# Level products of a block inverse on 32 columns instead of 64, with one masked buffer per level

## The chip, the cores and the metric

One core of a Trainium2 chip runs the whole program. The metric is the device time of one execution in microseconds, as the median of the runs shown. TensorE, VectorE, ScalarE and GpSimd each have their own instruction queue and meet only at semaphores: `wait_ge` holds an engine's queue until a counter is high enough, `then_inc` raises it when an instruction ends.

## The reference, cut to what matters

One layer of a streaming encoder is run on a prompt of 512 frames and a sample of 32. It has chunked attention (8 heads of 64), RWKV-7 time mixing (8 heads of 64), a gated merge and a feed-forward network. The change is in the time mixing, whose recurrence per head is

```
sa = -einsum('bhvk,bhk->bhv', S, kk_t)
S  = S * w_t + sa[..., None] * (kk_t * a_t) + v_t[..., None] * k_t
y_t = einsum('bhvk,bhk->bhv', S, r_t)
```

The state S after each frame depends on the state before it. The kernel doesn't step through frames. It takes chunks of 64 frames; inside a chunk all the `sa` follow from one triangular system with a 64x64 matrix, unit diagonal, and entries made of products of kk, a and the decays. The inverse of that matrix is what the level products compute.

## The kernel before, in words

**Stages.** First come the norm and the input projection in 21 units of weight columns (L1618 to L1693), all through float32r splits (`w_hi`, `w_lo`). Then, from about 339 to 560 us, comes the stage of the change. After it come the state's read-out, the two output projections, the merge and the feed-forward network.

**Units of the stage.** There are NT = 16 units: 4 head pairs (hp) times 4 tiles of 128 frames. A unit holds 2 heads (e) times 2 chunks of 64 frames (c). Chunk c sits on one half of the partitions (`part[c]`), head e on its own 64 columns. A 17th unit (n = NT) does the sample's frames in the same way with 4 levels. Everything of unit n is in buffer set q = n % 2, and its PSUM banks are `bank(q, 0)` to `bank(q, 2)`.

**The order of the stage** is written out by hand, in a loop on each engine over g = 0 .. 127, that is 8 rounds of 16 steps (L1294 on VectorE, L1863 on TensorE). A round takes two units a and b:
- steps 0 and 1: `p_scores` of each (the products that make the triangular matrices, and four transposes), then `v_masks` (L1194) with L1200, L1201, L1204;
- step 2: `p_cv`; step 3 to 12: five levels, each a P step and an X step, each first for a and then for b;
- step 13: `p_wu`, with X as weights; steps 14 and 15: `p_out` for each, and `v_out`.

After each step's work the engine issues a piece of attention (`p_attn`, `v_attn`): scores, transposes and value products of the head pair, 32 steps for each. That is all the filling between the levels. For each head pair after the first, GpSimd prepares the next pair's operands (`prelude`) beside the first round of a pair.

**The levels.** X starts as the inverse on 2x2 diagonal blocks. At level lev, with s = 2 << lev, neighbouring blocks of size s merge into blocks of 2s. In each block of 2s columns the first half is h = 0 and the second h = 1.
- P step (`p_level_p`, L1735): per e and c, one product with ATs as weights (64 columns) and X as moving operand (64 columns) into `bank(q, 2)`. 4 products.
- `v_level_p` (L1215): VectorE multiplies the result for both e by the level's mask into Pb. The mask `lmask[:, lev, :]` is nonzero only in the columns of h = 0. All 64 columns are written, the masked ones with zeros.
- X step (`p_level_x`, L1748): two products for each e and c: X transposed (XT) as weights with Pb moving, and Pb as weights with XT moving. They give the correction to X and to its transpose in `bank(q, 0)`. 8 products; at the last level only the second kind, 4.
- `v_level_x` (L1221): VectorE subtracts from X the columns of h = 0 and from XT those of h = 1, in place. These are all that a level changes.

The waits are a closed ring: the P step waits for `lev_x` of the level before, `v_level_p` for `lev_p_mm`, the X step for `lev_p`, `v_level_x` for `lev_x_mm`. TensorE does a's and b's step behind each other, so b's product runs while VectorE works on a.

A product is one `mm` (L1502, L1503). Matmul and weight load are separate instructions. A float32 product leaves two of each in the records. The two chunks use different quarters of the array and run side by side.

Of the kernel before, what the change touches and what calls it, by code (L numbers as in the profile page):

```python
# [20 lines left out]
ALU = mybir.AluOpType  # L21
AX = mybir.AxisListType.X

P = 128
# [26 lines left out]
def build(nc, x_prompt, x_sample, cache_k, cache_v, state_wkv, state_shift, c_prompt, c_sample, w_ada, b_ada,  # L51
# [6 lines left out]
    L = 64  # L58
# [21 lines left out]
    PERS, HH, HL, XT, RAW, HI, LO, ZS, E = 16512, 20224, 37760, 55296, 72832, 89216, 105600, 121984, 152736  # L80
# [5 lines left out]
    with ctx:  # L86
        def sem(name):
            return ctx.enter_context(nc.semaphore(name))
# [3 lines left out]
        at = lambda name, shape, offset, dt=F32: nc.alloc_sbuf_tensor_at(name, shape, dt, offset=offset)  # L92
# [28 lines left out]
        lmask = at("lmask", [P, 5, L], E + 70208)  # L121
# [32 lines left out]
        def made(q):  # L154
            def row(a, names):
                for n, c, w in names:
                    yield at(f"{n}{q}", [P, c, w], a)
                    a += 4 * c * w
            yield from row((HI, HL)[q], (
                ("ATs", 2, L), ("BDs", 4, L), ("CTs", 2, L), ("XX", 4, L), ("Pb", 2, L), ("KC", 2, P)))  # L160
            yield from row((LO, HL + 4608)[q], (("WU", 2, P), ("tk", 3, P)))
        ATs, BDs, CTs, XX, Pb, KC, WU, tk = zip(made(0), made(1))
        X, XT = [x[:, 0:2] for x in XX], [x[:, 2:4] for x in XX]
        SLOT1 = [a + 8192 + 2208 * i for a in (HI, LO, RAW) for i in range(3)]
        sets = [[at(f"{n}{q}", [P, W + (n == "E1")], a) for n, a in zip(("kt", "bh", "kh", "bl", "kl", "rt", "E1"), places)]
# [65 lines left out]
        hi_done, lo_done, unit_mm = sem("hi_done"), sem("lo_done"), sem("unit_mm")  # L231
# [18 lines left out]
        lev_p = [sem(f"lev_p{q}") for q in range(2)]  # L250
        lev_x_mm = [sem(f"lev_x_mm{q}") for q in range(2)]
        lev_x = [sem(f"lev_x{q}") for q in range(2)]
# [32 lines left out]
        U_OA = U_MG + NG  # L285
# [28 lines left out]
        part = [slice(0, DH), slice(DH, P)]  # L314

        def n_levels(n):

            return 5 if n < NT else 4

        def lev_at(n, lev):  # L320
            return 5 * (n // 2) + lev

        def bank(q, i):

            return ps[:, 3 * q + i, :]

        def squares(b, k, n):

            return b[:, k * L:(k + n) * L].rearrange("p (n c) -> p n c", n=n)

        def both_heads(q, k, n):

            return ps[:, 3 * q:3 * q + 2, k * L:(k + n) * L]

        def sample_out(hp):

            b = (5, 3, 4, 0)[hp]
            return ps[:, b, 256:256 + DH], ps[:, b, 256 + DH:256 + 2 * DH]
# [707 lines left out]
        def _(dve):  # L1046
            link = Chain(dve, dve_c)
            tt, sts, stt = dve.tensor_tensor, dve.tensor_scalar, dve.scalar_tensor_tensor
# [10 lines left out]
            for t, (c0, rows_) in enumerate(TILES):  # L1059
                q = t % 2  # L1060
# [154 lines left out]
            def v_level_p(n, lev):  # L1215
                q = n % 2
                dve.wait_ge(lev_p_mm[q], lev_at(n, lev) + 1)
                tt(Pb[q][:, :, :], squares(bank(q, 2), 4, 2), lmask[:, lev, :].unsqueeze(1).to_broadcast([P, 2, L]),  # L1218
                   ALU.mult).then_inc(lev_p[q], 1)

            def v_level_x(n, lev):  # L1221
                q, s = n % 2, 2 << lev
                dve.wait_ge(lev_x_mm[q], lev_at(n, lev) + 1)
                if lev < n_levels(n) - 1:
                    both = lambda x: bass.AP(tensor=x.tensor, offset=x.offset,
                                             ap=[list(x.ap[0]), [2 * L + s, 2], [2 * s, L // s], [1, s]])
                    x = both(XX[q][:, :, :])
                    tt(x, x, both(bank(q, 0)), ALU.subtract).then_inc(lev_x[q], 1)  # L1228
                else:
                    v = lambda a: a.rearrange("p u (b h s) -> p u b h s", h=2, s=s)[:, :, :, 1, :]  # L1230
                    tt(v(XT[q]), v(XT[q]), v(squares(bank(q, 0), 2, 2)), ALU.subtract).then_inc(lev_x[q], 1)

            def v_out(n):
                (hp, t), q = divmod(n, TT), n % 2
# [31 lines left out]
            def v_own(hp, e):  # L1266

                dve.wait_ge(own_mm, 2 * hp + e + 1)
                if hp:
                    dve.wait_ge(pt_mm, 2 * hp * KS)  # L1270
                low_of(s_sb[0:TS, e, T:T + TS], ps[0:TS, 7, e * TS:(e + 1) * TS],
                       bias[0:TS, hp * 2 + e, T - P:T - P + TS], HUGE, rsum[0:TS, e, 3:4]).then_inc(own_ev, 1)
# [10 lines left out]
            def v_attn(u):  # L1283
                hp, p = divmod(u, 32)
                if hp == HP:
                    return
                if head_at(p, 2, 1):
                    v_scale(hp, *head_at(p, 2, 1))
                if head_at(p, 0):
                    v_scores(hp, *head_at(p, 0))  # L1290
                if p in A_PV[0:2]:
                    v_own(hp, A_PV.index(p))

            for g in range(16 * NR_):  # L1294
                rnd, p = divmod(g, 16)
                a, b = 2 * rnd, 2 * rnd + 1
# [56 lines left out]
            for hp in range(HP):  # L1353
                om, on = sample_out(hp)
                stt(MT4[:, hp, :], dg2[:, :], e4[:, hp:hp + 1], om, ALU.mult, ALU.add)
                i = dve.tensor_copy(NN4[:, hp, :], on)
# [12 lines left out]
            for m in range(HP):  # L1369
# [4 lines left out]
                q = 2 * (m % 3)  # L1374
# [13 lines left out]
            for m in range(HP + 1):  # L1388
                if m < HP:
                    y, g = zs[:, 2 * HP + m, 1:W + 1], gring[:, (KD + m) % 3, :]  # L1390
                    o = sqy[m % 2]
# [40 lines left out]
            for k in range(KD):  # L1432
                i, j = k // 2, k % 2
# [7 lines left out]
                a = tmp_a[:, j, :]  # L1441
# [44 lines left out]
            for t, (_, rows_) in enumerate(TILES):  # L1486
                q = Y_PAIR[t]
                dve.wait_ge(ysq_done, t + 1)
                c = stat[0:rows_, t:t + 1]
# [5 lines left out]
                v = lambda a: a.rearrange("p (b c) -> p b c", b=2)  # L1495
# [5 lines left out]
        def _(pe):  # L1501
            def mm(out, lhsT, rhs, start=True, stop=True):  # L1502
                return pe.matmul(out, lhsT, rhs, start=start, stop=stop)  # L1503
# [11 lines left out]
            for t, (_, rows_) in enumerate(TILES):  # L1515
                if t >= 2:
                    pe.wait_ge(xt_free, t - 1)
                q = t % 2
                for k in range(KD):
                    o = ps[:, 2 * q + k // 4, (k % 4) * P:(k % 4) * P + rows_]  # L1520
                    i = pe.transpose(o, x_block(t, k), ident[0:rows_, 0:rows_])  # L1521
# [134 lines left out]
            for g in range(NG):  # L1656
# [8 lines left out]
                if g < HP:  # L1665
# [3 lines left out]
                    for h in range(2):  # L1669
                        for j in range(2):  # L1670
                            rank = slice(j * DH, (j + 1) * DH)
                            ins = mm(ps[:, 4 + 2 * j + h, 0:H], wup[rank, g * P:(g + 1) * P],
                                     zs[rank, ZT - 2, 1 + h * H:1 + (h + 1) * H])
# [9 lines left out]
                if g in (4, 5):  # L1683
                    for m in range(2 * g - 8, 2 * g - 6):
                        pe.wait_ge(kksq, m + 1)
                        for h in range(2):
                            ins = mm(ps[32 * h:32 * h + 32, 4, 0:H], ind[:, m, :], pz[:, m % 2, h * H:(h + 1) * H],
                                     m == 0, m == HP - 1)
# [46 lines left out]
            def p_level_p(n, lev):  # L1735
                q = n % 2
                if lev == 0:
                    pe.wait_ge(x0_done, n + 1)
                    pe.wait_ge(at_ev, n + 1)
                    pe.wait_ge(cv_ev, n + 1)  # L1740
                else:
                    pe.wait_ge(lev_x[q], lev_at(n, lev))
                for e in range(2):
                    for c in range(2):
                        ins = mm(bank(q, 2)[part[c], (4 + e) * L:(5 + e) * L], ATs[q][part[c], e, :], X[q][part[c], e, :])
                ins.then_inc(lev_p_mm[q], 1)

            def p_level_x(n, lev):  # L1748
                q = n % 2
                pe.wait_ge(lev_p[q], lev_at(n, lev) + 1)  # L1750
                o = bank(q, 0)
                for e in range(2):
                    if lev < n_levels(n) - 1:
                        for c in range(2):
                            mm(o[part[c], e * L:(e + 1) * L], XT[q][part[c], e, :], Pb[q][part[c], e, :])
                    for c in range(2):
                        ins = mm(o[part[c], (2 + e) * L:(3 + e) * L], Pb[q][part[c], e, :], XT[q][part[c], e, :])
                ins.then_inc(lev_x_mm[q], 1)

            def p_wu(n):  # L1760
# [102 lines left out]
            for g in range(16 * NR_):  # L1863
                rnd, p = divmod(g, 16)
                a, b = 2 * rnd, 2 * rnd + 1
# [72 lines left out]
            ins = p_chunks(0, [slice(32 * hp, 32 * hp + 32) for hp in range(HP)], *zip(*[sample_out(hp) for hp in range(HP)]))  # L1938
# [11 lines left out]
            for m in range(HP):  # L1950
                q = 2 * (m % 3)
# [7 lines left out]
                for e in range(2):  # L1959
                    ins = mm(ps[part[e], q + 1, 0:TS], SS[part[e], NCH + 1, m, :], zs[part[e], m, 1 + S0:1 + W])  # L1960
                ins.then_inc(y_mm, 1)

            for m in range(HP):
# [4 lines left out]
                b = 2 * ((m + 1) % 3)  # L1968
                for h in range(2):
                    ins = mm(ps[:, b + h, 0:H], bones[:, :], zs[:, 2 * HP + m, 1 + h * H:1 + (h + 1) * H])  # L1970
# [3 lines left out]
            for m in range(HP):  # L1974
                pe.wait_ge(ysq, m + 1)
                for h in range(2):
                    ins = mm(ps[32 * h:32 * h + 32, 4, 0:H], ind[:, m, :], sqy[m][:, h * H:(h + 1) * H],
                             m == 0, m == HP - 1)
# [57 lines left out]
            for k in range(KD):  # L2036
# [3 lines left out]
                for t, m in enumerate((1, 0)):  # L2040
                    c = k * UW + m * P
                    for j, (w, x) in enumerate(((w_hi, hh), (w_hi, hl), (w_lo, hh))):
                        for h in range(2):
                            ins = mm(ps[:, 2 * t + h, 0:H], w[:, U_UP % 2, c:c + P],
                                     x[:, k, h * H:(h + 1) * H], k == 0 and j == 0, k == KD - 1 and j == 2)
# [25 lines left out]
            u, n = U_DN + 2 * KD - 2, T_DN + KD - 1  # L2071
# [3 lines left out]
            for h in range(2):  # L2075
                for c in range(KDN):
                    hi, lo = ah[:, KDN + c, h * H:(h + 1) * H], al[:, KDN + c, h * H:(h + 1) * H]
                    for j, (w, x) in enumerate(((w_hi, hi), (w_hi, lo), (w_lo, hi))):
                        ins = mm(ps[:, 2 + h, 0:H], w[:, (U_DN + 1) % 2, c * P:c * P + P], x, False, c == KDN - 1 and j == 2)
# [42 lines left out]
```

## Time and profile before

| | us |
|---|---|
| median of 3 runs (1108.6 to 1109.32) | 1108.92 |
| the profiled execution | 1111.06 |
| its span, from first to last instruction | 1109.1 |

| engine | busy us | share |
|---|---|---|
| TensorE, matmul | 1049.9 | 95% |
| TensorE, weight load | 973.4 | 88% |
| VectorE | 393.1 | 35% |
| ScalarE | 346.1 | 31% |
| GpSimd | 369.7 | 33% |

Busy time is the union of an engine's instructions. A matmul's record includes its way through the array, so the TensorE figure isn't the share of its peak. The granted clock (PEclk) is 1 where TensorE ran at 2.4 GHz and 0.5 where it ran at 1.2 GHz; a value between is a mean over a stretch. The mean over the whole run was 0.981.

### The profile page before, as it was taken

The numbers are of one execution on the slowest core, as the hardware profiler recorded it, in microseconds if no ns is written. First come the engines' busy times: TensorE is split into PE (matmuls) and PEld (weight loads), VectorE is DVE, ScalarE is ACT, GpSimd is POOL, SyncE is SP. The second block draws the span as 40 slices with busy tenths as digits, with TensorE's granted clock in tenths as the row PEclk, the third lists the DMA queues.
The fourth block names the chain that finished last, engine by engine and source line by source line (L and its number), as shares of the span: only waits on it lengthen the run. The fifth ranks groups of instructions, "written<-read, shape, count | busy, mean of one in ns | idle before, by whom it ended". The sixth has DMA issues, their size and how long they took to land.

```text
span 1109.1 us, 25395 instructions
## 1 busy us (share of the span) xinstructions
PE 1049.9 (95%) x11052; PEld 973.4 (88%) x11052; DVE 393.1 (35%) x912; ACT 346.1 (31%) x614; POOL 369.7 (33%) x252
## 2 busy tenths in 40 slices
PE   6899999999998989888898899999999999999996
PEld 5699999999997767776796899999999999999996
DVE  2500000086036666666547766322222222100003
ACT  4521222243333444444232323322322232211112
POOL 0555443343315060500231142343343334343340
PEclk9899999999999989899998999999999999999999
DMA  9786756233411000021242432223322322232312
GB/s 368 259 274 232 266 198 205 95 123 132 138 42 46 12 12 22 3 98 76 78 138 72 127 95 77 77 76 105 84 76 76 108 80 64 60 98 82 100 53 81
DMA packets 117180, 122.21 MB, mean 110 GB/s; under 512 B 5428, under 2 KB 102880, under 8 KB 113640
## 3 DMA queue, kind: packets, MB, share of 16 engines
q1 hardware_dynamic: 111872, 111.86, 31.3%
q10 hardware_dynamic: 5224, 9.10, 2.5%
q8 instruction: 69, 1.13, 0.4%
q14 instruction: 15, 0.12, 0.0%
HBM read 108.33 MB, written 15.23 MB: 111 GB/s over the span
## 4 chain that ended last, share of the span: by engine, by line
PE 87%; DVE 8%; issue 2%; ACT 1%; POOL 1%; DMA 1%; SPq 0%; DVEq 0%; ACTq 0%; POOLq 0%
PE ps L1503 83%; PE ps L1823 2%; DVE s_sb L1247 1%; DMA xtok_s<-in_x_sample 1%; PE ps L1723 1%; POOL w_lo L579 1%; DVE y_sb L1496 1%; DVE s_sb L1281 1%; PE ps L1521 1%; DVE mt L1418 0%; DVE Pb L1218 0%; DVE XX L1228 0%; DVE sqy L1395 0%; DVE sq_a L1092 0%; DVE sqy L1399 0%
## 5 line engine op out<-in xcount | busy, mean ns | idle before, releaser
L579 POOL TENSOR_TENSOR w_lo<-w_raw,w_hi 128x2048 fp32r<-128x2048 f32 (+1 forms) x67 | 287.2, 4287 | 565.1 <-ACT w_hi L728 565.1
L1503 PE MATMUL ps<-hh,w_hi 128*128 128x274 f32 x1376 | 291.5, 293 | 5.4 <-DVE hl L1097 4.0
L1503 PE MATMUL ps<-hh,w_lo 128*128 128x274 f32 x1376 | 289.6, 292 | 0.0
L1503 PE MATMUL ps<-hl,w_hi 128*128 128x274 f32 x1376 | 288.1, 291 | 0.0
L1503 PEld LDWEIGHTS ps<-hh,w_hi 128*128 128x128 f32 x1376 | 219.6, 190 | 13.9 <-issue 11.5
L1503 PEld LDWEIGHTS ps<-hl,w_hi 128*128 128x128 f32 x1376 | 219.5, 190 | 0.0
L1503 PEld LDWEIGHTS ps<-hh,w_lo 128*128 128x128 f32 x1376 | 219.2, 191 | 0.0
L728 ACT ACTIVATE w_hi<-w_raw 128x2048 fp32r<-128x2048 f32 (+1 forms) x67 | 119.3, 1781 | 105.0 <-PE ps L1503 99.2
L1503 PE MATMUL ps<-ah,w_hi 128*128 128x274 f32 x352 | 75.3, 290 | 0.3 <-POOL w_lo L579 0.3
L1503 PE MATMUL ps<-ah,w_lo 128*128 128x274 f32 x352 | 75.5, 291 | 0.0
L1503 PE MATMUL ps<-al,w_hi 128*128 128x274 f32 x352 | 75.3, 290 | 0.0
L1503 PEld LDWEIGHTS ps<-ah,w_hi 128*128 128x128 f32 x352 | 56.5, 189 | 0.5 <-POOL w_lo L579 0.5
L1503 PEld LDWEIGHTS ps<-ah,w_lo 128*128 128x128 f32 x352 | 56.6, 190 | 0.0
L1503 PEld LDWEIGHTS ps<-al,w_hi 128*128 128x128 f32 x352 | 56.5, 190 | 0.0
L1024 ACT ACTIVATE ah<-ff_a 128x548 f32 (+1 forms) x22 | 14.6, 662 | 133.8 <-DVE ff_a L1465 133.8
L1461 DVE TENSOR_TENSOR ff_a<-ps,rstd 128x548 f32<-128x548 f32 x22 | 16.0, 728 | 113.7 <-PE ps L1503 113.6
L1428 DVE SCALAR_TENSOR_TENSOR xT<-ps,mod,xT 128x274 f32<-128x274 f32 (+1 forms) x15 | 7.5, 501 | 108.1 <-PE ps L1503 108.1
L1503 PE MATMUL ps<-XX,Pb 64*64 64x64 f32 x672 | 41.8, 228 | 2.6 <-DVE Pb L1218 2.6
L1503 PEld LDWEIGHTS ps<-XX,ATs 64*64 64x64 f32 x672 | 26.2, 145 | 17.9 <-issue 10.4
L1503 PE MATMUL ps<-Pb,XX 64*64 64x64 f32 x536 | 37.7, 236 | 3.0 <-DVE Pb L1218 1.7
L657 POOL TENSOR_TENSOR oal<-qk,oah 128x548 fp32r<-128x548 f32 x4 | 5.4, 1356 | 104.6 <-ACT oah L932 104.6
L1503 PE MATMUL ps<-XX,ATs 64*64 64x64 f32 x672 | 33.9, 238 | 6.6 <-ACT KC L878 3.0
(356 smaller groups left out, 1479.6 us busy)
## 6 DMA issues: line engine op xcount, KB each, us to landing
w_raw<-in_w_ffn_in SPq DMA_DIRECT2D x44, 512.0 KB, 4.7
w_raw<-in_w_in SPq DMA_DIRECT2D x42, 512.0 KB, 5.0
ada_l<-in_w_ada SPq DMA_DIRECT2D x16, 1024.0 KB, 6.3
ada_w<-in_w_ada SPq DMA_DIRECT2D x8, 1024.0 KB, 14.1
w_raw<-in_w_ffn_out SPq DMA_DIRECT2D x16, 384.0 KB, 4.0
gring<-g_d SPq DMA_DIRECT2D x20, 274.0 KB, 2.9
w_raw<-in_w_ffn_out SPq DMA_DIRECT2D x16, 320.0 KB, 3.4
g_d<-gst SPq DMA_DIRECT2D x16, 274.0 KB, 2.6
```

Source lines behind the costliest of these rows:

```text
L579: pool.tensor_tensor(w_lo[:, s, 0:cols], w_raw[:, s, 0:cols], w_hi[:, s, 0:cols].bitcast(F32), ALU.subtract).then_inc(lo_done, 1)
L728: act.activation(w_hi[:, s, 0:cols], w_raw[:, s, 0:cols], ACT.Copy).then_inc(hi_done, 1)
L1024: act.activation(ah[:, i - U_UP, :], ff_a[:, :], ACT.Copy).then_inc(ah_done, 1)
L1247: return dve.tensor_tensor_reduce(out=out, in0=x, in1=y, scale=-1.0, scalar=first, op0=ALU.add, op1=ALU.min, accum_out=low)
L1281: sts(v, v, rsum[0:rows_, e, 2:3], None, ALU.mult).then_inc(p_scaled, 1)
L1428: link(stt(xa[:, 0:H], ps[:, 2 * q, 0:H], g(0), xa[:, 0:H], ALU.mult, ALU.add))
L1461: tt(halves(ff_a[:, :]), pair(1), halves(rstd2[:, :]), ALU.mult).then_inc(pair_free, 1)
L1496: stt(v(y_sb[0:rows_, t, :]), ps[0:rows_, 2 * q:2 * q + 2, :], c, v(gf_row[0:rows_, :]), ALU.mult, ALU.mult).then_inc(yt_done, 1)
L1503: return pe.matmul(out, lhsT, rhs, start=start, stop=stop)
L1521: i = pe.transpose(o, x_block(t, k), ident[0:rows_, 0:rows_])
L1723: ins = pe.transpose(bank(q, 2)[:, i * P:(i + 1) * P], x, ident[:, :])
L1823: ins = pe.transpose(ps[:, 6 + e, b * rows_:(b + 1) * rows_], s_sb[0:rows_, e, b * P:(b + 1) * P], ident[0:rows_, 0:rows_])
```

## The change

The changed code does the following.

- P step: the moving operand is `half(X, lev, 0)`, the 32 columns of h = 0, picked with a stepped access pattern. The results lie densely, 32 columns for each e, in PSUM.
- `v_level_p`: reads the 32 dense columns for each e, multiplies by the half of the mask, and writes only the columns of h = 0 of a masked buffer.
- Each level has a masked buffer of its own, `Pl[q][lev]`; level 0 uses the old Pb. The columns of h = 1 are cleared once, before the loop, by VectorE (10 memsets of 128x2x64, behind a wait for the 21 units of the input projection), and nothing writes them after that.
- X step: the first kind moves the 32 columns of h = 0 of the masked buffer, with all 64 columns of XT as weights. The second kind has all 64 columns of the masked buffer as weights and moves the 32 columns of h = 1 of XT. Results are again dense.
- `v_level_x`: same elements of X and XT as before; the PSUM operand is dense.

The new buffers use space behind the units' small tiles (HI + 4608) and at RAW.

```
+        Pl = [[Pb[q]] + [at(f"Pl{q}{lev}", [P, 2, L], a + 512 * (lev - 1)) for lev in range(1, 5)]
+              for q, a in enumerate((HI + 4608, RAW))]
...
+        def half(x, lev, h):
+            return x.rearrange("p (b h s) -> p b h s", h=2, s=2 << lev)[:, :, h, :]
...
 def v_level_p(n, lev):
-                tt(Pb[q][:, :, :], squares(bank(q, 2), 4, 2), lmask[:, lev, :].unsqueeze(1).to_broadcast([P, 2, L]),
-                   ALU.mult).then_inc(lev_p[q], 1)
+                sides = lambda x: x.rearrange("p e (b h s) -> p e b h s", h=2, s=2 << lev)[:, :, :, 0, :]
+                m = half(lmask[:, lev, :], lev, 0)
+                tt(sides(Pl[q][lev][:, :, :]), bank(q, 2)[:, 4 * L:5 * L].rearrange("p (e b s) -> p e b s", e=2, s=2 << lev),
+                   m.unsqueeze(1).to_broadcast([P, 2] + list(m.shape[1:])), ALU.mult).then_inc(lev_p[q], 1)
...
 before the loop of VectorE
+            dve.wait_ge(unit_mm, U_OA)
+            for b in Pl[0] + Pl[1]:
+                i = dve.memset(b[:, :, :], 0.0)
+            link(i)
...
 def p_level_p(n, lev):
-                        ins = mm(bank(q, 2)[part[c], (4 + e) * L:(5 + e) * L], ATs[q][part[c], e, :], X[q][part[c], e, :])
+                        ins = mm(bank(q, 2)[part[c], 4 * L + 32 * e:4 * L + 32 * e + 32], ATs[q][part[c], e, :],
+                                 half(X[q][part[c], e, :], lev, 0))
...
 def p_level_x(n, lev):
-                            mm(o[part[c], e * L:(e + 1) * L], XT[q][part[c], e, :], Pb[q][part[c], e, :])
+                            mm(o[part[c], 32 * e:32 * e + 32], XT[q][part[c], e, :], half(b[part[c], e, :], lev, 0))
-                        ins = mm(o[part[c], (2 + e) * L:(3 + e) * L], Pb[q][part[c], e, :], XT[q][part[c], e, :])
+                        ins = mm(o[part[c], L + 32 * e:L + 32 * e + 32], b[part[c], e, :], half(XT[q][part[c], e, :], lev, 1))
```

`mm(out, lhsT, rhs)`: the second argument is the weights, the third moves.

## Rows read from the trace of the kernel before

**Rows 1.** The page: granted clock in 40 slices; the chain by line.
```profile
PEclk9899999999999989899998999999999999999999
...
PE ps L1503 83%; PE ps L1823 2%; DVE s_sb L1247 1%; DMA xtok_s<-in_x_sample 1%; PE ps L1723 1%; POOL w_lo L579 1%; DVE y_sb L1496 1%; DVE s_sb L1281 1%; PE ps L1521 1%; DVE mt L1418 0%; DVE Pb L1218 0%; DVE XX L1228 0%; DVE sqy L1395 0%; DVE sq_a L1092 0%; DVE sqy L1399 0%
```

**Rows 2.** Instructions on tile XX; names are out<-moving,weights; duration min/median/max ns, first and last start.
```profile
L1503 PE MATMUL ps<-XX,ATs x672: 217/219/367, 345.3 to 549.1; 64*64 64x64 f32 x168
...
L1503 PE MATMUL ps<-XX,Pb x672: 217/218/312, 346.3 to 551.6; 64*64 64x64 f32 x168
...
L1503 PE MATMUL ps<-Pb,XX x536: 213/219/367, 346.2 to 547.7; 64*64 64x64 f32 x179
...
L1228 DVE TENSOR_TENSOR XX<-XX,ps x67: 268/286/293, 347.4 to 548.1; 128x128 f32<-128x128 f32 x67
...
L1231 DVE TENSOR_TENSOR XX<-XX,ps x17: 201/220/222, 359.4 to 551.9; 128x64 f32<-128x64 f32 x17
```

**Rows 3.** Instructions on tile lmask, the masked copy.
```profile
L1218 DVE TENSOR_TENSOR Pb<-ps,lmask x84: 268/290/293, 345.8 to 549.3; 128x128 f32<-128x128 f32 x84
```

**Rows 4.** Windows: the level stretches, busy us of each engine, clock, DMA.
```profile
345.20:360.90 15.70, 15.44 (x268) 11.87 (x270) 9.26 (x40) 4.55 (x15) 11.12 (x12) 0.89 0.01 3
370.00:384.90 14.90, 13.53 (x263) 10.18 (x260) 10.34 (x42) 4.79 (x12) 0.00 (x0) 1.00 0.07 20
395.00:411.50 16.50, 15.56 (x256) 11.88 (x258) 10.00 (x41) 3.61 (x13) 13.36 (x21) 0.79 0.01 3
...
447.20:463.10 15.90, 15.44 (x246) 12.04 (x247) 8.52 (x32) 3.08 (x10) 11.76 (x20) 0.73 0.01 3
...
497.50:511.20 13.70, 12.17 (x247) 9.45 (x248) 7.45 (x34) 3.08 (x10) 0.00 (x0) 1.00 0.50 208
...
sum 118.20, PE 109.91 PEld 85.24 DVE 74.51 ACT 35.36 POOL 41.00; mean PE 13.74 PEld 10.65 DVE 9.31 ACT 4.42 POOL 5.12
```

**Rows 5.** The same eight windows, instructions on tile XX alone.
```profile
sum 118.20, PE 75.54 PEld 64.06 DVE 20.61; mean PE 9.44 PEld 8.01 DVE 2.58
```

**Rows 6.** Waits from 339 to 543 us: total us, times, longest.
```profile
PEld ps L1503 <- DVE Pb L1218: 10.0, 20, 0.8
...
PE ps L1503 <- DVE Pb L1218: 4.2, 9, 0.6
```

**Rows 7.** The chain in order of time: start us, us, what, records.
```profile
386.57 3.12 PE ps L1503 x156
...
396.61 1.08 PE ps L1503 x32
...
447.22 1.90 PE ps L1503 x32
```

**Rows 8.** TensorE in order of time: start us, us; rows*columns of weights, rows x moving columns.
```profile
345.29 0.68 PE L1503 MATMUL ps<-XX,ATs 64*64 64x64 f32 x16 [1.69 <-ACT KC L878]
...
387.36 0.66 PE L1503 MATMUL ps<-pt_sb,vcs 128*64 128x32 f32 x16
```

**Rows 9.** In order of time before the first mask; a VectorE memset by form.
```profile
338.45 0.10 POOL L653 MEMSET E<- 128x1 f32 x1 [21.24 <-PE ps L1503]
...
340.70 0.29 DVE L1200 TENSOR_TENSOR CTs<-ps,strictU 128x128 f32<-128x128 f32 x1 [3.43 <-PE ps L1723]
...
L1051 DVE MEMSET sc<- 128x256 f32 x1 | 0.3, 272 | 0.9 <-PEq L2106 0.9
```

**Rows 10.** Windows of 5 us around two falls of the clock, and one without.
```profile
380.00:385.00 5.00, 4.03 (x85) 2.71 (x80) 4.75 (x21) 1.71 (x5) 0.00 (x0) 1.00 0.01 3
440.00:445.00 5.00, 3.77 (x88) 2.80 (x80) 4.53 (x11) 3.95 (x15) 3.54 (x3) 1.00 0.17 50
445.00:450.00 5.00, 3.94 (x52) 3.19 (x54) 3.63 (x13) 1.55 (x5) 4.78 (x7) 0.54 0.00 0
...
590.00:595.00 5.00, 2.31 (x16) 1.22 (x14) 4.06 (x6) 0.72 (x2) 0.00 (x0) 1.00 0.28 64
595.00:600.00 5.00, 2.87 (x10) 1.92 (x10) 4.47 (x7) 1.13 (x2) 0.00 (x0) 0.56 0.36 104
```

More of the change, by code:

```diff
@@ L1224, in v_level_x @@
                 if lev < n_levels(n) - 1:
[L1225 to L1228, printed above, removed]
-                else:
-                    v = lambda a: a.rearrange("p u (b h s) -> p u b h s", h=2, s=s)[:, :, :, 1, :]
-                    tt(v(XT[q]), v(XT[q]), v(squares(bank(q, 0), 2, 2)), ALU.subtract).then_inc(lev_x[q], 1)
+                    x = XX[q][:, :, :]
+                    x = bass.AP(tensor=x.tensor, offset=x.offset,
+                                ap=[list(x.ap[0]), [2 * L + s, 2], [2 * s, L // s], [1, s]])
+                    tt(x, x, bank(q, 0)[:, 0:2 * L].rearrange("p (u b s) -> p u b s", u=2, s=s), ALU.subtract)\
+                        .then_inc(lev_x[q], 1)
+                else:
+                    x = XT[q].rearrange("p e (b h s) -> p e b h s", h=2, s=s)[:, :, :, 1, :]
+                    tt(x, x, bank(q, 0)[:, L:2 * L].rearrange("p (e b s) -> p e b s", e=2, s=s), ALU.subtract)\
+                        .then_inc(lev_x[q], 1)
             def v_out(n):
@@ L1750, in p_level_x @@
                 pe.wait_ge(lev_p[q], lev_at(n, lev) + 1)
-                o = bank(q, 0)
+                o, b = bank(q, 0), Pl[q][lev]
                 for e in range(2):
```

## The prediction

> **What bounds the kernel now.** I read the page first. TensorE carries 83% of the chain that ended last, by one line, L1503, the helper through which every product goes, and its granted clock is full in most slices, with short falls in and just before the middle of the run [rows 1]. The changed code runs only in the stage from 339 to 560 us, so I then asked for that stage alone. There the view by tile gives the level products: 672 records that have X as moving operand against ATs, 536 that move the masked buffer and 672 that hold it, each 64 columns wide, in all 1880 records, two for each of 940 products, as every float32 product leaves two [rows 2]. The same view gives the VectorE side: 84 masked copies of 290 ns, 67 subtractions of 286 ns and 17 of 220 ns [rows 2, 3].
>
> The windows over the eight level stretches (each serves two units) say what the stage waits for. The eight take 118.2 us; TensorE is busy for 109.9 of it, VectorE for 74.5 [rows 4]. 75.5 us of TensorE's are products with XX [rows 5], so 34.4 us are other work: attention's scores, transposes and value products that the written order puts between the levels. TensorE bounds the stretches, and VectorE's latency opens short gaps: 29 waits for the masked copy, 10.0 + 4.2 = 14.2 us together [rows 6].
>
> The views of time and of the chain say what one step costs. The X step of two units is 32 records in 1.08 us where the clock is full, and 1.90 us in a stretch at the lower one [rows 7]. The first stretches of three of the four head pairs had a mean clock of 0.89, 0.79 and 0.73 and took 15.7, 16.5 and 15.9 us; the first stretch of the last head pair kept 1.00 and took 13.7; so did the second stretch of every pair, of which one is shown [rows 4]. At 1 for 2.4 GHz and 0.5 for 1.2 GHz those means are 2 x (0.11 x 15.7 + 0.21 x 16.5 + 0.27 x 15.9) = 19 us at 1.2 GHz, and they cost up to 2.0 + 2.8 + 2.2 = 7.0 us.
>
> **The change, part by part.** Nothing is removed from TensorE's list: 940 products, 1880 records, 940 pairs of weight loads, all still there. Each moves 32 columns instead of 64. The weights stay 64 columns wide: ATs, X transposed, and the masked buffer, whose untouched half must be zero because all 64 of its columns are still loaded; that is what the fixed zeros are for.
>
> *The products at full clock.* The trace has a near twin of the new form, attention's 128x32 products with 64 weight columns, also two tiles side by side: 16 records in 0.66 us. Sixteen level records of 64 moving columns take 0.68 us [rows 8]. Half the stream bought 0.02 us per group, and it is bought once, at an end of the group, since in between a pair waits for its weights. So the products themselves gain nothing in their middle. Bounds: 0, or the pace of the stream, 0.54 us less per 32 records; I take 0.02 us for each group that someone waits for, since the twin has the same two counts of columns.
>
> The Trainium skill (TensorE: Matmul & The Clock Gate, section LDWEIGHTS) says that a weight load takes time by its columns alone. [...]
>
> *VectorE.* The masked copy goes from 128 to 64 elements a partition. L1231 is a 128x64 operation on the same operands: 220 ns against 290 [rows 2, 3]. That is 70 ns x 84 = 5.9 us of VectorE's time, which is worth nothing where TensorE is busy. It is on the path at the 29 waits: 29 x (0.07 + 0.02) = 2.6 us, and the next thing late there is the product before it. Bounds: 0 and 5.9; I take -2. The subtractions keep their 128 and 64 elements; the source is now dense and not strided: 0. The half-view that writes or streams runs of 2 to 32 elements is not in the trace for TensorE; the nearest are VectorE's strided subtractions at the price of the dense masked copy, 286 against 290 ns, so 0, up to a few microseconds if TensorE minds short runs.
>
> *The clearing.* Ten memsets of 128x128 stand on VectorE behind a new wait for the last of the input projection's 21 units, which GpSimd's L653 waits for too, until 338.45 us [rows 9]. Behind them is the first mask, for which TensorE waits. That mask starts at 340.70, after 3.43 us of idle time. A memset of 128x256 took 272 ns, so ten of half the size are at most 1.4 to 2.7 us, in a gap of 2.25 [rows 9]. GpSimd copies small tiles in the same gap and could hold VectorE up. Cost 0; if the cover goes, about +1.
>
> *The clock.* This is the term that decides. What TensorE did before it fell is in the windows: from 440 to 445, at full clock, it was busy 3.77 of 5 us with 88 records, then ran 445 to 450 at 0.54. From 380 to 385 it was busy 4.03 us with 85 records and kept the clock, and so did the following stretch [rows 10]. So level stretches stand close to where the clock falls. Now 69% of TensorE's work in them (75.5 of 109.9) has its stream halved. If a shorter stream counts as less work, more of the level stretches run at 1.2 GHz. The trace has neither the case nor its size: bounds are the 19 us at 1.2 GHz of now and the whole 118 us. I take 60 us, half of it, since the steps with attention's wide scores between them still look as they do now, and those without look emptier than what preceded a fall.
>
> What that costs is not what it costs now. A level product with 32 columns at 1.2 GHz streams as long as one of 64 at 2.4 GHz, which its weights hide (if the loads are not slower there; else up to the 1.90 us of today). So levels cost 1.08 us per step at either clock, and only the other work doubles. (a) 41 us more at 1.2 GHz, in which other work is 34.4 of 118.2, that is 0.29 at full clock: 41 / 1.29 x 0.29 = +9. Bounds 0 and +34. (b) The low clock outlives the last level step and reaches the W/U and output products, which are dense: 156 records in 3.12 us [rows 7]. In half of the eight rounds for some 3 us, of which 1.5 is lost: 4 x 1.5 = +6; bounds 0 and 8 x 3.1 = +25. (c) In the 19 us that are already low the level products stop paying: 0.69 x 7.0 = -4.8; some of the 7.0 is GpSimd's and VectorE's shared time, so -4; bounds 0 and -7.
>
> The Trainium skill's same page (HAM oscillation) says that the gate takes the clock away after too little activity and that the penalty then comes on every round. The falls in the trace agree in kind; no row here shows that columns are what it counts.
>
> **Sum.** +9 + 6 - 4 - 2 + 0 = +9 us. The profiled execution took 1111.06 us with a span of 1109.1; what lies around the span stays, so it would be 1120. The median of the runs shown is 1108.92, 2.1 below it, so the forecast is 1108.92 + 9 = 1118.
>
> **Rivals.**
> 1. *The clock stays as it is* (the gate does not mind shorter streams). Then only (c) and VectorE's term are left: -4 - 2, 1103 us. For it: the fall after 595 us came behind 5 us in which TensorE was busy for only 2.31, emptier than any level stretch [rows 10]. Against it: the level stretches with 246 to 268 records at 0.73 to 0.89 are not empty, and fell.
> 2. *The products follow their columns.* 1880 records are 940 pairs at 1.08 / 16 = 0.068 us; half of it on some 60% of the pairs that bound, 0.034 x 940 x 0.6 = -19, with the two gains of rival 1: 1084 us. Against it: 0.66 against 0.68 us [rows 8].
> 3. *Clock and gains cancel*: 1.2 GHz for only some 20 us more, (a) +4.5, (b) +2, less 6: 1109 us.
> 4. *The clearing is not covered*: GpSimd's copies, and its longer operations after, hold each memset, and the first round is late by 3 us while the clock stays: 1106. It matters only beside another case.
>
> **How the numbers follow.** The forecast has 0.6, rival 1 has 0.21, rival 2 has 0.05, rival 3 has 0.12, rival 4 has 0.02. The forecast's own range is 1112 to 1128 by its bounds' nearer halves; the clock falling nearly everywhere would give 1108.92 + 20 to 25. To hold 8 in 10 the range reaches over rival 3 and into rival 1: 1102 to 1127. About 0.2%, 2.2 us, can be told from no change. Faster by more: rivals 1, 2 and 4 and a little of the third, 0.28. Within: 0.14. Slower: 0.58.
>
> **What would show it.** PEclk in the eight level stretches: mean well under 0.9 in most of them, also in the second stretch of each head pair, which is 1.00 now. If these keep 1.00, the clock theory is wrong. The X step of 32 records should still be about 1.08 us at full clock; 0.6 would be rival 2. At the low clock it should be near 1.1 and not 1.9. The masked copy should read 220 ns. The first mask should still start near 340.7. The forecast is wrong in size if the time at 1.2 GHz is far from 60 us in these stretches, or if that time costs less than 0.2 us for each microsecond of it.

## The result, and the profile after

The changed kernel takes 1136.93 us (median of 4 runs, 1135.34 to 1145.82), the kernel before 1109.12 beside it. The ratio is 1.0252, 95% interval 1.022 to 1.0283: slower by 2.5%, some 28 us. The forecast was 1118, slower by 9 us; the sign and the cause held, the size was a third. The profiled execution took 1135.37 us with a span of 1133.7, which is 24.6 us longer than before. TensorE's mean granted clock fell from 0.981 to 0.950.

The page after, granted clock in 40 slices; it answers to [rows 1]:

```profile
PEclk9999999999995969696999899999999999999999
```

There are four dents, one for each head pair; the shallow fifth, the 8 in slice 23, has its like in slice 22 of the kernel before. The windows after, over the eight level stretches: length, then busy us (and records) of TensorE, weight load, VectorE, ScalarE and GpSimd, then the clock. Each stretch runs from a round's first P product to its first W/U product:

```profile
344.30:367.40 23.10, 22.51 (x260) 17.18 (x260) 9.32 (x39) 4.55 (x14) 12.32 (x20) 0.50 0.01 2
378.90:392.90 14.00, 12.69 (x265) 10.32 (x263) 9.87 (x42) 4.78 (x11) 0.00 (x0) 1.00 0.05 15
401.70:423.30 21.60, 19.38 (x256) 14.94 (x256) 10.71 (x41) 4.68 (x15) 14.45 (x22) 0.59 0.01 2
434.50:448.40 13.90, 12.60 (x262) 10.24 (x261) 9.81 (x42) 4.78 (x11) 0.00 (x0) 1.00 0.04 12
459.80:479.40 19.60, 18.68 (x254) 14.58 (x254) 9.51 (x41) 4.61 (x15) 13.62 (x21) 0.59 0.01 2
490.10:505.60 15.50, 14.19 (x263) 11.40 (x261) 9.79 (x42) 4.78 (x11) 0.00 (x0) 0.89 0.05 13
514.50:533.20 18.70, 18.19 (x256) 14.27 (x256) 8.09 (x40) 3.57 (x12) 0.00 (x0) 0.60 0.45 185
544.10:557.10 13.00, 11.70 (x260) 9.54 (x259) 9.17 (x40) 6.59 (x12) 4.67 (x1) 1.00 0.01 3
sum 139.40, PE 129.94 PEld 102.48 DVE 76.28 ACT 38.34 POOL 45.06; mean PE 16.24 PEld 12.81 DVE 9.53 ACT 4.79 POOL 5.63
```

The stretches of [rows 4] were cut a little differently, so here is the kernel before with the new cut, the four first stretches, one second stretch and the sum:

```profile
345.30:360.40 15.10, 14.93 (x258) 11.33 (x259) 8.78 (x39) 4.45 (x15) 10.63 (x11) 0.89 0.01 3
370.70:385.10 14.40, 13.03 (x265) 10.33 (x263) 10.38 (x42) 4.78 (x11) 0.00 (x0) 1.00 0.04 12
393.90:411.00 17.10, 15.52 (x256) 11.71 (x256) 10.68 (x41) 4.71 (x15) 14.39 (x22) 0.80 0.01 3
...
444.40:462.60 18.20, 16.52 (x254) 12.60 (x254) 10.90 (x41) 4.67 (x15) 14.40 (x22) 0.72 0.01 2
...
496.00:510.70 14.70, 12.64 (x254) 9.70 (x254) 8.54 (x40) 3.64 (x13) 0.00 (x0) 1.00 0.58 236
...
sum 121.70, PE 110.72 PEld 85.88 DVE 79.66 ACT 38.40 POOL 44.17; mean PE 13.84 PEld 10.74 DVE 9.96 ACT 4.80 POOL 5.52
```

The two have the same products, and their record counts differ by three at most in a stretch. The four first stretches grew by 8.0, 4.5, 1.4 and 4.0 us and ran at 0.50 to 0.60. The second stretches at full clock got shorter, 14.4 to 14.0 us: that is what the change earns where the clock doesn't move. From clock and length, 2 x (1 - clock) x length, the level stretches now have 75 us at 1.2 GHz against 20. That is 55 more for 17.7 us of length, 0.32 us lost for each. The rest of the 24.6 us, 6.9, lies outside the level stretches. 6.1 of it is in the gaps between the stretches, which had a clock of 1.00 before and have some 16 us at 1.2 GHz now. The gap that grew most, by 2.6 us, is this one:

```profile
448.40:459.80 11.40, 10.67 (x248) 9.17 (x246) 4.85 (x17) 6.01 (x27) 3.65 (x3) 0.70 0.09 26
```

The chain after, in order of time (start, us, line, records), shows the price of one X step and of the output products:

```profile
345.74 1.85 PE ps L1518 x32
...
394.34 3.12 PE ps L1518 x156
...
449.89 5.40 PE ps L1518 x156
...
461.72 1.05 PE ps L1518 x32
```

An X step of 32 records takes 1.05 us at full clock and 1.85 at the low one, where 64 columns took 1.08 and 1.90 [rows 7]. Half the stream is worth 3% at either clock. The output products took 3.12 us at full clock and 5.40 in a fall. The windows of the same stretches confirm the clock:

```profile
345.74:347.59 1.85, 1.85 (x33) 1.78 (x33) 0.87 (x3) 0.30 (x2) 1.79 (x4) 0.50 0.00 0
461.72:462.77 1.05, 1.05 (x33) 0.94 (x32) 1.05 (x2) 0.28 (x1) 0.99 (x2) 1.00 0.00 0
449.89:455.29 5.40, 5.40 (x158) 5.04 (x158) 1.47 (x8) 1.83 (x13) 0.00 (x0) 0.50 0.18 52
```

VectorE's side after, by tile, and then in order of time before the first mask:

```profile
L1226 DVE TENSOR_TENSOR Pl<-ps,lmask x67: 201/225/227, 348.6 to 572.3; 128x64 f32<-128x64 f32 x67
```

```profile
338.40 0.58 DVE L1306 MEMSET Pl<- 128x128 f32 x4
339.65 0.29 DVE L1206 TENSOR_TENSOR CTs<-ps,strictU 128x128 f32<-128x128 f32 x1 [0.66 <-PE ps L1738]
```

The masked copy takes 225 ns, not 290. The clearing ends at 338.98 (338.40 + 0.58) and the first mask still waits 0.66 us for TensorE: it costs nothing.

### The profile page after: what moved, and what is told of

Read it like the earlier page. It is cut to its first block, busy times and chain, and to the rows that moved or that the text cites. A ratio compares the mean times of both kernels' runs of the same rounds, so it can differ in the third digit from the quotient of the medians.

```text
span 1133.7 us, 25406 instructions
## 1 busy us (share of the span) xinstructions
PE 1075.5 (95%) x11052; PEld 996.0 (88%) x11052; DVE 389.5 (34%) x922; ACT 346.2 (31%) x614; POOL 370.2 (33%) x252
## 4 chain that ended last, share of the span: by engine, by line
PE 86%; DVE 7%; issue 2%; DMA 2%; SPq 1%; ACT 1%; POOL 1%; DVEq 0%; ACTq 0%; POOLq 0%
PE ps L1518 83%; PE ps L1839 2%; DMA ada_w<-in_w_ada 2%; SPq L445 1%; DVE s_sb L1257 1%; PE ps L1738 1%; DVE s_sb L1291 1%; POOL w_lo L585 1%; DVE y_sb L1511 1%; DVE mt L1433 0%; DVE XX L1236 0%; DVE sq_a L1098 0%; DVE gring L1431 0%; DVE hl L1103 0%; PE ps L1627 0%
## 5 line engine op out<-in xcount | busy, mean ns | idle before, releaser
L1518 PEld LDWEIGHTS ps<-hh,w_hi 128*128 128x128 f32 x1376 | 218.8, 190 | 14.2 <-issue 10.5
L1518 PEld LDWEIGHTS ps<-XX,ATs 64*64 64x64 f32 x672 | 30.5, 166 | 18.3 <-issue 12.3
L1518 PE MATMUL ps<-XX,ATs 64*64 64x32 f32 x672 | 36.4, 250 | 6.6 <-ACT KC L884 2.9
L1518 PE MATMUL ps<-XX,Pl 64*64 64x32 f32 x536 | 39.7, 255 | 2.4 <-DVE Pl L1226 2.4
## 6 DMA issues: line engine op xcount, KB each, us to landing
ada_w<-in_w_ada SPq DMA_DIRECT2D x8, 1024.0 KB, 14.1
```

## The experiments

The first three experiments test the cause against a rival: A, shorter streams take the clock down; B, VectorE's new work costs the time.

**e1: full streams, everything else of the change.** The edit, in part in words:

```
 def p_level_p   (changed kernel)
-    mm(bank(q, 2)[part[c], 4 * L + 32 * e:4 * L + 32 * e + 32], ATs[q][part[c], e, :], half(X[q][part[c], e, :], lev, 0))
+    mm(bank(q, 2)[part[c], (4 + e) * L:(5 + e) * L], ATs[q][part[c], e, :], X[q][part[c], e, :])
 def v_level_p
-    source: bank(q, 2)[:, 4 * L:5 * L], dense
+    source: sides(squares(bank(q, 2), 4, 2))
 def p_level_x
-    both kinds move half(..., lev, h)
+    both kinds move all 64 columns; v_level_x as before
```

> The changed kernel with the streams of all level products put back to 64 columns; the masked buffers with fixed zeros, their clearing and VectorE's masked copy of 64 elements stay. Theory A (the shorter streams lower the granted clock): the clock of the stage returns to about 0.95 to 1.00, the X step of 32 records is 1.08 us there, and the time is that of the kernel before less up to 3 us for the shorter masked copy: 1106 to 1109 us. Theory B (the cost is VectorE's: clearing, stepped writes, more buffers): it stays at 1130 us or more, since all of that is still in.

Measured: 1108.11 us, ratio 0.9993 (0.9979 to 1.0008), mean clock 0.981. Theory B is out: the clearing, the masked buffers and VectorE's shorter copy are all still in. The level stretches of e1, the four first ones and the sum:

```profile
347.00:362.00 15.00, 14.86 (x260) 11.46 (x260) 8.52 (x39) 4.54 (x14) 10.59 (x11) 0.89 0.01 3
...
395.20:411.10 15.90, 14.04 (x254) 10.66 (x254) 10.61 (x41) 4.70 (x15) 14.34 (x22) 0.89 0.01 3
...
444.30:461.30 17.00, 15.19 (x255) 11.67 (x255) 10.58 (x41) 4.66 (x14) 14.32 (x22) 0.80 0.01 2
...
494.40:507.50 13.10, 12.45 (x256) 9.59 (x256) 8.09 (x40) 3.65 (x13) 0.00 (x0) 1.00 0.66 267
...
sum 116.40, PE 107.23 PEld 83.86 DVE 76.41 ACT 38.49 POOL 44.00; mean PE 13.40 PEld 10.48 DVE 9.55 ACT 4.81 POOL 5.50
```

**e2 and e3: one step at a time.** e2 is e1 with the P step's 32 columns of the change; e3 is e1 with the X step's.

> The changed kernel with 32 columns in the P step alone (336 of 940 products); the X step streams 64. Theory A, with the stream as what counts: about a third of the dose, so the clock between 0.95 and 0.98 over the whole run and a time of 1110 to 1122 us; with steps, as the clock has two levels only, it need not be in proportion. Theory B: 1130 us or more, with the clock of the changed kernel.

> The changed kernel with 32 columns in the X step alone (604 of 940 products); the P step streams 64. Theory A: about two thirds of the dose: 1118 to 1132 us, more than the variant with the P step alone. Theory B: as the changed kernel, 1130 us or more, and no different from the P step alone.

Measured: e2 1117.97 us, ratio 1.0092 (1.0047 to 1.0138); e3 1129.2 us, 1.0171 (1.0143 to 1.02). The order and the sizes are A's. The sum over the level stretches and the longest of them, first of e2, then of e3:

```profile
445.40:465.20 19.80, 17.73 (x256) 13.87 (x256) 10.49 (x41) 4.66 (x14) 14.39 (x22) 0.66 0.01 2
...
sum 121.10, PE 111.58 PEld 88.14 DVE 75.66 ACT 38.33 POOL 44.11; mean PE 13.95 PEld 11.02 DVE 9.46 ACT 4.79 POOL 5.51
```

```profile
451.20:472.90 21.70, 20.20 (x256) 15.65 (x256) 10.22 (x41) 4.72 (x15) 14.40 (x22) 0.56 0.01 2
...
sum 136.20, PE 127.06 PEld 99.51 DVE 76.17 ACT 38.42 POOL 44.05; mean PE 15.88 PEld 12.44 DVE 9.52 ACT 4.80 POOL 5.51
```

In the four kernels with these masked buffers the span rises with the time at 1.2 GHz. Time at 1.2 GHz in the whole span, 2 x (1 - mean clock) x span, against the span:

| kernel | mean clock | span us | at 1.2 GHz | over e1: span / low time |
|---|---|---|---|---|
| e1, streams of 64 | 0.981 | 1105.5 | 42 | |
| e2, P step 32 | 0.972 | 1111.8 | 62 | 6.3 / 20 = 0.31 |
| e3, X step 32 | 0.954 | 1127.4 | 104 | 21.9 / 62 = 0.35 |
| changed, both 32 | 0.950 | 1133.7 | 113 | 28.2 / 71 = 0.40 |

The price isn't quite constant, 0.31 to 0.40. Single executions agree: the slowest of e2 had a clock of 0.955 and a span of 1126.5 us, nearly those of e3's profiled one, 0.954 and 1127.4. The same clock goes with the same span, whichever step has the short stream.

One rival stands untested. In every run with 32 moving columns they are picked by a stepped pattern, so their number and the step weren't changed apart. The step doesn't slow the products (1.05 against 1.08 us), but no run here moved 32 adjacent columns.

**e4 and e11: more work to hold the clock.** e4 adds to the changed kernel, e11 the same to the kernel before, in the first round of each head pair:

```
 p_level_p: for _ in range(4 if lev == 0 and n in (0, 1, 4, 5, 8, 9, 12, 13) else 1):   # the 4 products
 loop:      after the P step of b at levels 1 to 4: mm(ps[:, 1, 320:512], ident[:, :], bias[:, 0, 0:192])
            (left out in one place, g = 9)
```

The repeated P products move 32 columns in e4 and 64 in e11.

> The changed kernel with more work for TensorE, in the first round of each head pair: the P products of level 0 are issued four times instead of once, and behind the P step of each later level stands one product of 192 columns whose result nobody reads. That is about 4 x (4 x 0.32 + 2 x 0.7) = 11 us more of TensorE's work at full clock, some of it in gaps. Theory A: the clock of these rounds rises from 0.50 to 0.76 towards 1, and the time falls though there is more work: 1115 to 1128 us. Theory B, or any cause that is not the clock: the time rises by 5 to 11 us, to 1140 or more.

> The price of the added work: the kernel before with the same additions as the changed kernel had in the filler experiment (level 0's P products four times in the first round of each head pair, one product of 192 columns behind the P step of later levels). That experiment took 1142.3 us against 1136.9, 5 us more. If the clock gave nothing back there, the additions cost the same 5 us here: 1114 us. If it gave something back, they cost more here: 1118 to 1125 us, and the difference over 5 us is what the clock gave back.

Measured: e4 1142.26 us (1136.59 to 1153.87), ratio 1.0326 (1.0265 to 1.0387), mean clock 0.956; e11 1112.57 us, 1.0027 (1.0012 to 1.0042), 0.989. e4 missed A's range and lies where B, or any cause that isn't the clock, had put it. e11 missed both of its ranges: the additions cost 2.5 us there (1112.57 against 1110.12 beside it), not 5 or more. In the changed kernel they lifted the clock from 0.950 to 0.956 only. B is out by e1, so e4 leaves the clock as the cause standing, since it hardly moved the clock, but it doesn't support it either. It gave no gain; that it is slower than the changed kernel isn't shown, since the intervals of the two ratios overlap (1.022 to 1.0283 for the changed kernel).

**e10: the changed kernel, more work at the thin start alone** (the same repetition of P at level 0 for the first three head pairs, and p_cv of the second unit three times).

> The changed kernel with the same repeated products at the thin starts. Theory E (the thin start alone takes the clock down and the short streams only keep it down): most of the loss goes, 1112 to 1122 us. Theory F (the short streams in the level steps take it down by themselves): the clock falls one or two steps later, and the time is 1130 to 1138 us.

Measured: 1137.9 us, 1.0255 (1.0228 to 1.0283), mean clock 0.948: no change in the time, as F had it. But the trace isn't F's. The two level stretches of its second head pair:

```profile
406.80:420.40 13.60, 13.42 (x308) 10.90 (x303) 9.31 (x41) 4.83 (x15) 13.05 (x18) 1.00 0.02 5
430.60:451.10 20.50, 19.70 (x263) 15.56 (x261) 10.28 (x42) 4.78 (x11) 0.00 (x0) 0.59 0.03 10
```

The first kept 1.00 from end to end, with short streams, in 13.6 us; the changed kernel had 0.59 and 21.6 us there. The fall came one round later, at 0.59 for 20.5 us, in a second stretch that the changed kernel ran at 1.00. So the repeated products moved a fall and did not save it. Level steps with short streams held the clock in one place and lost it in others; the runs don't say which condition decides.

**e5 and e6: the pace of a product, by weights and stream.** In both, ATs, XT and the masked buffer are loaded with `[part[c], e, 0:32]`; e5 moves 32 columns, e6 64. Both leave out half of the rows of each result, and VectorE's correction is a comparison in place of the subtraction, so the inverse isn't computed.

> A measurement of the product's pace, in the changed kernel: every level product has 32 columns of weights and moves 32 columns. Half of the rows of each result are not computed, and VectorE's correction of X is a comparison instead of the subtraction, so the inverse is not computed and only the pace of an X step of 32 records is read. Theory C (the 64 columns of weights set the pace at either clock): the step falls from 1.05 us at full clock to about 0.6, and at the low clock from 1.85 us to about 1.0. Theory D (a fixed cost per product sets it): 1.05 and 1.85 stay.

> The same measurement with 32 columns of weights and 64 moving columns, again with only half of the rows of each result and a comparison in place of the subtraction. Theory C has the pace set by the wider of the two: 1.05 to 1.08 us at full clock, about 1.85 at the low one, as with 64 and 64. The granted clock should be near that of the kernel before, 0.98, as the streams are the same; if it is 0.95 as in the changed kernel, it is the loaded columns and not the moved ones that go with the clock.

Measured, in one execution each: 1110.4 and 1104.68 us, mean clock 0.962 and 0.980. X steps of 32 records, the chain of e5:

```profile
456.50 1.00 PE ps L1519 x32
...
503.25 0.63 PE ps L1519 x32
```

and of e6:

```profile
345.98 1.85 PE ps L1517 x32
355.04 1.01 PE ps L1517 x32
```

The windows of e5 over its two steps give their clock, 0.50 and 1.00:

```profile
456.50:457.50 1.00, 1.00 (x34) 0.94 (x34) 0.69 (x2) 0.38 (x1) 1.00 (x3) 0.50 0.00 0
503.25:503.88 0.63, 0.63 (x33) 0.59 (x34) 0.44 (x2) 0.38 (x1) 0.00 (x0) 1.00 0.88 360
```

and those of e6, also 0.50 and 1.00:

```profile
345.98:347.83 1.85, 1.85 (x34) 1.68 (x33) 0.86 (x3) 0.32 (x3) 1.79 (x4) 0.50 0.00 0
355.04:356.05 1.01, 1.01 (x34) 0.86 (x33) 0.97 (x5) 0.38 (x1) 0.93 (x2) 1.00 0.06 16
```

Together with the two kernels, one X step of 32 records:

| weight columns / moving columns | at 2.4 GHz | at 1.2 GHz |
|---|---|---|
| 64 / 64 (before) | 1.08 us | 1.90 us |
| 64 / 32 (changed) | 1.05 | 1.85 |
| 32 / 64 (e6) | 1.01 | 1.85 |
| 32 / 32 (e5) | 0.63 | 1.00 |

Theory C holds: the wider of weights and stream sets the pace, at either clock, and D, a fixed cost, is out. The clock went with the stream: e6, which loads 32 columns and moves 64, kept 0.980, while the changed kernel, which loads 64 and moves 32, has 0.950. This rests on single executions of e5 and e6; the kernel before lay between 0.977 and 0.984 in 23 executions beside them. e5 had 0.962 and was still faster than the changed kernel, since its steps at the low clock cost what the others' cost at the full one.

**e7, e8 and e9: the other way round.** The clock also falls in the kernel before, at the start of a head pair, where TensorE waits for VectorE. These repeat products in front of such waits, in rounds 0, 2 and 4:

```
 p_level_p: for _ in range(4 if lev == 0 and n in (0, 1, 4, 5, 8, 9) else 1):   # e7 and e8 on e1, e9 on before
 p_cv:      for _ in range(3 if n in (1, 5, 9) else 1):                         # e8 and e9
```

> The variant with full streams and the shorter masked copy (1108.1 us), plus activity in a gap: in the first rounds of the first three head pairs the P products of level 0 are issued four times (0.7 us more for each unit, while VectorE is held at L1210 and TensorE would wait). If the clock's falls there (13.7 us in that variant's profile, some 0.33 us lost for each us) come from the thin start of the round, half of them go: 1105 to 1107 us. If not, the time is the same or up to 1 us more.

> As the one before, and in the same rounds the second unit's p_cv products are issued three times (0.47 us more, also in front of a wait). If the thin start is what takes the clock down: the clock stays at 1.00 through these rounds in most executions, 1103 to 1106 us. Rival: the repeated products hold up ScalarE's copies of the result, and the time is 1108 to 1111 us.

> The kernel before, with nothing of the change, and the repeated products at the thin start of the first three head pairs (P products of level 0 four times, p_cv of the second unit three times). If all of the 4 us gained by the variant with them came from the clock, this has 1105 to 1107 us; what is left to the variant's 1105.0 is the shorter masked copy's, 0 to 2 us. If the two gains need each other, it stays at 1108 to 1110.

Measured: e7 1107.15 us, 0.9975 (0.9958 to 0.9991); e8 1104.99 us, 0.9952 (0.9937 to 0.9967); e9 1106.35 us, 0.9969 (0.9952 to 0.9986). Mean clocks 0.984, 0.985, 0.988. e7 ended just above its range, e8 and e9 inside theirs. The first stretches of e8's first three head pairs and its sum:

```profile
344.70:361.10 16.40, 16.26 (x306) 12.92 (x306) 8.41 (x39) 4.55 (x14) 10.52 (x11) 0.90 0.02 4
...
394.40:408.90 14.50, 14.05 (x304) 11.02 (x304) 10.56 (x41) 4.94 (x15) 13.87 (x20) 1.00 0.02 5
...
442.00:456.50 14.50, 14.07 (x304) 11.05 (x302) 10.55 (x41) 4.95 (x15) 13.87 (x20) 1.00 0.02 4
...
sum 114.00, PE 107.48 PEld 84.99 DVE 76.30 ACT 38.94 POOL 43.02; mean PE 13.43 PEld 10.62 DVE 9.54 ACT 4.87 POOL 5.38
```

With 48 records of repeated P products more in each of these stretches the second and third take 14.5 us, against 15.9 and 17.0 in e1, which is e8 without the repetition, and 17.1 and 18.2 before. The first stretch still fell once. e8 beats both kernels; e9 shows that most of it, 0.3 of the 0.5%, needs nothing of the change. The last 0.2% is the size of the masked copy's gain, and the two intervals overlap, so that share isn't shown.

## Why the prediction was right in sign and wrong in size

- *Streams don't pace the products at full clock* (0.02 us for a group): right. 1.08 became 1.05 us, and rival 2 would have shown 0.6.
- *The masked copy, -2 us*: right in kind, 225 ns against the 220 forecast. The three second stretches that kept full clock show the change's whole gain there, 0.4 or 0.5 us each; over eight stretches that would be some 3 us. e1, which has the copy but not the short streams, got most of it: 14.1 us in each of the first three second stretches, against 14.4. Its level stretches take 116.4 us against 121.7, but with less time at 1.2 GHz than before. The working had a slip: it took 14.2 us of waits as gaps of TensorE, but its matmuls stood idle for only 118.2 - 109.9 = 8.3 us of the stretches. 10.0 of the 14.2 were waits of the weight loads, in part while products still ran. The size came out in spite of that.
- *The clearing, 0*: right.
- *More of the level stretches at 1.2 GHz, 60 us in place of 19*: right in kind, mis-sized: 75 us by the clocks above. It was also laid on the wrong stretches. I expected the second stretches of each head pair to fall too; three of four kept 1.00, and the four first ones were low for most of their length, with mean clocks of 0.50 to 0.60. The prediction had named just this, second stretches at 1.00, as the sign that the clock theory is wrong. The theory held, by e1, so the sign was badly chosen, and that the total came near is in part luck.
- *"So levels cost 1.08 us per step at either clock, and only the other work doubles"*: this is the step that failed. The sum took the weight load's time as fixed and only the stream as slowed by the clock. The bracket beside it, "else up to the 1.90 us of today", was the truth: 1.85 us at the low clock, where the prediction said near 1.1 and not 1.9. With it, term (c), -4, is 0: the 20 us that were already low got no cheaper. And term (a), +9, has all of TensorE's work in it and not 0.29 of it. The rate that [rows 4] gave, 7.0 us lost in 19, 0.37 for each us at 1.2 GHz, was the one to use: by the 55 us more that were measured it gives 20. The stretches grew by 17.7, VectorE's gain of some 3 included. The rate was on the page and was argued away.
- *The carry past the last level, (b), +6*: right in size, half right in kind. 6.9 us of the growth lie outside the level stretches. The four gaps behind first stretches grew by 1.2, 1.0, 0.5 and 0.7 us, 3.4 together, and these were carried. The largest piece, 2.6 us with output products at 5.40 us in place of 3.12, lies behind a second stretch that kept 1.00: a fall of its own, not a carry. The agreement with 6 is in part luck.
- With (a) at 20, (b) at 6, (c) at 0 and VectorE at -2 the sum is 24 us; the span grew by 24.6. This is a sum made afterwards, from measured times at 1.2 GHz.
- *Range*: it ended at 1127, by the nearer halves of its bounds. The far ends, +34 for (a) and +25 for (b), were worked out from rows too, and a range that has to hold should have reached further towards them.

The rule that I weighed, the Trainium skill's on weight loads by columns alone (TensorE: Matmul & The Clock Gate, section LDWEIGHTS), agrees with the runs at full clock: halving only the stream gave 1.05, halving both 0.63 us. But by columns alone the step of 64 loaded and 32 moved columns would take the same time at either clock. It took 1.05 us at 2.4 GHz and 1.85 at 1.2 GHz. With 32 loaded columns it took 1.00 us at 1.2 GHz, so it wasn't the stream that held the 1.85 up; there the measurement decides.

## What to carry to other kernels

Before cutting the moving side of small products, look at the weight side: in this kernel the wider of the two set the pace, and half a stream over full weights was worth 3% of the step. Then look at the granted clock in the stretch: here a stage that already dipped to 1.2 GHz lost more clock when its streams were cut, and each microsecond more at that level cost 0.3 to 0.4 us. Price such a stretch with what the dips cost in the trace at hand, for all of TensorE's work, and try the opposite too: repeating cheap products in front of a wait made the kernel before 0.3% faster (e9), and 0.5% together with the shorter masked copy (e8).

## What the runs showed of the hardware

- A float32 product with 64 columns of weights and 32 moving, or 32 and 64, runs within 7% of the pace of 64 and 64, at both clocks (the table above). Only with both at 32 did it run clearly faster: 0.63 us in place of 1.05 for a step, and 1.00 in place of 1.85.
- Work that nobody needs can shorten the time: 48 more records in a stretch, 14.5 us in place of 15.9 (e8 against e1), and 0.3% off the whole time of the kernel before (e9). In the changed kernel the same kind of addition, its P products with 32 moving columns, only moved a fall (e10, mean clock 0.948).
- With the columns of the level products' streams halved, and as many products as before, the mean granted clock fell from 0.981 to 0.950.
- Not settled: how much of the falling clock would come back if the level steps were short in both weights and stream with the inverse still computed. e5 says that such steps cost 1.00 us even at the low clock, but it left half of the rows out.
